# Conditioning vectors in PSUM banks 4 to 7 beside the first projections, and value transposes taking turns with the probability transposes

## The reference

```python
mod_x = silu(c) @ w_ada[l] + b_ada[l]        # 6 x 1024 values: shifts, scales, gates
mod_c = silu(c_ctx) @ w_ada[l] + b_ada[l]    # the same for the context tokens
hx = modulate(rmsnorm(x_lat, g_attn[l]), sh1x, sc1x)
aqx, akx, avx, bqx, bkx, bvx = split_cols(hx @ w_in[l])
# group A: 8 query heads on 2 key/value heads of 64, q and k rms-normalised, rotated
# group B: 4 heads, two 64-wide softmax maps each, values of 128, softmax(1) - lam * softmax(2)
x_lat = x_lat + g1x * (merge_heads(a_out_x, b_out_x, g_sub[l], lam_init) @ w_o[l])
# then an up-projection, a convolution of width 3, SiLU gate, a down-projection
```

## Time and profile before

| | us |
|---|---|
| median of 3 runs | 1796.95 |
| lowest and highest | 1795.91, 1799.62 |
| the profiled execution | 1795.55 |
| its span in the trace | 1793.7 |

### The profile page before, as it was taken

One profiled execution on the slowest core, in us unless ns is written; L12 is line 12 of the kernel. 1 busy time (PEld: TensorE's weight loads), 2 busy tenths in 40 slices (PEclk: granted clock), 3 DMA queues, 4 the chain that ended last, 5 costly groups with the idle time before them and its releaser, 6 DMA issues.

```text
span 1793.7 us, 26070 instructions
## 1 busy us (share of the span) xinstructions
PE 1674.4 (93%) x9610; PEld 1418.3 (79%) x9610; DVE 1135.6 (63%) x1744; ACT 768.8 (43%) x1267; POOL 629.8 (35%) x311
## 2 busy tenths in 40 slices
PE   5869998889999999999999998999878999999997
PEld 3757877668888888888888886787767888888887
DVE  6996767667877566667336674677654864254256
ACT  6526666445244321333123344665545443243242
POOL 0454652121113334322433317564122154444442
PEclk9988999899999999999999999999999999999999
DMA  9340000023313243343434422001012132332222
GB/s 387 113 139 24 24 25 24 13 92 147 103 50 127 83 138 119 114 132 110 157 109 130 152 94 93 16 24 35 24 35 88 54 106 94 103 96 94 94 94 94
DMA packets 45534, 168.24 MB, mean 94 GB/s; under 512 B 4736, under 2 KB 6784, under 8 KB 43520
## 3 DMA queue, kind: packets, MB, share of 16 engines
q1 hardware_dynamic: 40896, 156.48, 25.9%
q10 hardware_dynamic: 4544, 10.49, 1.6%
HBM read 161.71 MB, written 5.24 MB: 93 GB/s over the span
## 4 chain that ended last, share of the span: by engine, by line
PE 78%; DVE 11%; issue 5%; ACT 3%; DMA 2%; POOL 1%; SPq 0%; ACTq 0%; DVEq 0%; POOLq 0%
PE ps L1193 22%; PE ps L1194 22%; PE ps L1195 22%; PE ps L1315 4%; PE ps L1329 3%; DVE junk_lead L1990 2%; PE ps L1348 2%; DVE nb L2266 1%; PE ps L1349 1%; DVE p_sb L2284 1%; DVE pt_lo L2291 1%; PE ps L1139 1%; DMA ada_first<-first_d 1%; POOL w_lo L1075 1%; DVE ht L2105 1%
## 5 line engine op out<-in xcount | busy, mean ns | idle before, releaser
L1075 POOL TENSOR_TENSOR w_lo<-w_raw,w_hi 128x1024 fp32r<-128x1024 f32 x175 | 446.9, 2556 | 939.6 <-ACT w_hi L1588 939.5
L1193 PE MATMUL ps<-h_hi,w_hi 128*128 128x512 f32 (+1 forms) x1592 | 566.8, 356 | 9.4 <-DVE h_lo L2113 6.9
L1194 PE MATMUL ps<-h_lo,w_hi 128*128 128x512 f32 (+1 forms) x1592 | 556.5, 350 | 0.0
L1195 PE MATMUL ps<-h_hi,w_lo 128*128 128x512 f32 (+1 forms) x1592 | 556.0, 349 | 0.0
L1193 PEld LDWEIGHTS ps<-h_hi,w_hi 128*128 128x128 f32 x1592 | 303.1, 190 | 57.2 <-issue 19.0
L1195 PEld LDWEIGHTS ps<-h_hi,w_lo 128*128 128x128 f32 x1592 | 302.6, 190 | 39.7
L1194 PEld LDWEIGHTS ps<-h_lo,w_hi 128*128 128x128 f32 x1592 | 303.3, 191 | 35.9
L1588 ACT ACTIVATE w_hi<-w_raw 128x1024 fp32r<-128x1024 f32 x188 | 198.3, 1056 | 246.9 <-PE ps L1195 218.7
L1193 PE MATMUL ps<-a_hi,w_hi 128*128 128x512 f32 (+1 forms) x552 | 191.6, 347 | 1.2 <-DVE a_lo L2480 1.2
L1194 PE MATMUL ps<-a_lo,w_hi 128*128 128x512 f32 (+1 forms) x552 | 191.3, 347 | 0.0
L1195 PE MATMUL ps<-a_hi,w_lo 128*128 128x512 f32 (+1 forms) x552 | 191.0, 346 | 0.0
(11 more groups left out here) (173 smaller groups left out, 2467.1 us busy)
## 6 DMA issues: line engine op xcount, KB each, us to landing
w_raw<-w_d SPq DMA_DIRECT2D x188, 512.0 KB, 3.5
ada_b<-ada_d SPq DMA_DIRECT2D x56, 512.0 KB, 4.3
ada_first<-first_d SPq DMA_DIRECT2D x8, 1024.0 KB, 21.9
ada_lead<-ada_d SPq DMA_DIRECT2D x14, 512.0 KB, 3.5
ada_mid<-ada_d SPq DMA_DIRECT2D x10, 512.0 KB, 7.2
x_sb<-x_d SPq DMA_DIRECT2D x2, 1536.0 KB, 11.0
x_sb<-x_d ACTq DMA_DIRECT2D x1, 3072.0 KB, 11.4
x_spill_d<-x_sb ACTq DMA_DIRECT2D x1, 2048.0 KB, 7.5
```

The source lines that it names most:

```text
L1075: nc.gpsimd.tensor_tensor(w_lo[:, c % RING, :], w_raw[:, c % RAW, :], w_hi[:, c % RING, :].bitcast(f32), ALU.subtract).then_inc(w_lo_done, 1)
L1193: nc.tensor.matmul(out, lh, rh, start=first, stop=False)
L1194: nc.tensor.matmul(out, lh, rl_, start=False, stop=False)
L1195: return nc.tensor.matmul(out, ll, rh, start=False, stop=last)
```

## The change

1. **Conditioning in PSUM, layer 0.** ScalarE's silu moves into the loop of the first norm (`conditioning(k)`), a half at a time, with the table load at k = 1 and the spill at k = 4. It then copies each silu'd vector, 1024 columns, to PSUM: `c_held(0)` in banks 4 and 5 (k = 5), `c_held(1)` in banks 6 and 7 (k = 7). The 28 instructions of VectorE (`ada_ahead`) read the vector from there. The tiles have four buffers instead of two; the third and fourth lie where `c_bc` was, so their first loads wait for the spill and for both copies. SP's order of tile and unit loads is LEADS_AHEAD.
2. **Banks and order of the opening.** In layer 0 units 2 to 6 rotate over banks 0 to 2, head squares go to bank 3, and the values of A are transposed in bank 2 alone. Head factors wait for the last conditioning tile. All tiles have positions from -20 up, and SD, SR, RH, RL have -25 instead of -6, in both layers.
3. **Value transposes in turns, both layers.** `turn_beside` gives the two parts of a head B's value transposes two numbers in the sequence of T, so they use banks 4 and 5 in turn with the probability transposes. They come after the last T of item 0 for head 0, of A's last item with j = 2 for head 1, and of the last item of head B 0 and of head B 1 for heads 2 and 3 (`behind`), and before the first T of the item after it. Bank 7 holds projections alone. The operations of units 9 to 11 are made after A's items with j = 2 instead of after all of A.

```diff
+LEADS_AHEAD = [2, 2, 2, 3, 2, 3]
-def unit_banks(u):
+def unit_banks(l, u):
+    if l == 0:
+        return {0: (0, 1), 1: (2, 3), 2: (0, 1), 3: (2, 0), 4: (1, 2), 5: (0, 1), 6: (0, 1)}.get(u, (7, 7))
     return {0: (0, 1), 1: (2, 3), 2: (4, 5), 3: (6, 7), 4: (0, 1), 5: (2, 3), 6: (0, 1)}.get(u, (7, 7))
...
+    last_j = {j: [it["n"] for it in items if it["kind"] == "A" and it["j"] == j][-1] for j in range(A_HEADS // 2)}
+    behind = [0, last_j[2], at_b[1] - 1, at_b[2] - 1]
...
-            ada.append(op("DVE", "ada", 2.35, -20 + (c - 2 * KT) * .5, [], c=c))
+            ada.append(op("DVE", "ada", 2.6, -20 + (c - 2 * KT) * .5, [], c=c))
...
-            ada.append(op("DVE", "ada", 2.6, -3, [ada[-1]], c=c))
+            ada.append(op("DVE", "ada", 2.6, -20 + (c - 2 * KT) * .5, [ada[-1]], c=c))
-    sd = op("ACT", "SD", 1.7, -6, [y["ST"] for y in normed])
-    rc = op("DVE", "SR", 1.7, -6, [sd])
-    rh = op("ACT", "RH", .4, -6, [rc])
-    both = op("DVE", "RL", .45, -6, [rh])
+    sd = op("ACT", "SD", 1.7, -25, [y["ST"] for y in normed])
+    rc = op("DVE", "SR", 1.7, -25, [sd])
+    rh = op("ACT", "RH", .4, -25, [rc])
+    both = op("DVE", "RL", .45, -25, [rh])
-    bank_user = {0: units[2]["SQ"] + units[2]["EV"], 1: units[3]["SQ"] + units[3]["EV"]}
+    bank_user = {0: ada[-1:], 1: ada[-1:]}
+    if l > 0:
+        bank_user = {0: units[2]["SQ"] + units[2]["EV"], 1: units[3]["SQ"] + units[3]["EV"]}
...
-            turn_values(y, (7, 7), 0)
-            y["VH"][0]["need"] += home(y)
-            raw_free[u % 2] = [y["VT"][-1]]
+            raw_free[u % 2] = y["VT"] = []
+    def turn_beside(y, it):
+        nonlocal n_t
+        y["VH"], y["VL"] = [], []
+        for n, (k0, k1) in enumerate([(0, 4), (4, 6)]):
+            tid = n_t
+            n_t += 1
+            at = it["n"] + .9 + .05 * n
+            lo2, v2 = t_ops[tid - 2]["LOT"], v_ops[tid - 2]
+            vt = op("PE", "VT", .11 * (k1 - k0), at, y["EV"] + [lo2, it["T"][-1]] + y["VT"][-1:], y=y, n=n, k0=k0, k1=k1,
+                    bank=4 + tid % TURNS, before=dict(lo2=lo2))
+            vh = op("ACT", "VH", .62 if n == 0 else .4, at, [vt] + (home(y) if n == 0 else []), y=y, n=n, VT=vt, k0=k0, k1=k1,
+                    bank=4 + tid % TURNS)
+            vl = op("DVE", "VL", .68 if n == 0 else .42, at, [vh], y=y, n=n, VH=vh, k0=k0, k1=k1, bank=4 + tid % TURNS)
+            vt["LOT"] = vl
+            t_ops[tid], v_ops[tid] = vt, v2
...
+        for b in range(B_HEADS):
+            if behind[b] == n - 1:
+                turn_beside(units[B_TILE + 3 * b + 1], prev_item)
...
+    lead_home = [R_QKV + 28 * KB, R_QKV + 32 * KB, R_X + 24 * KB, R_X + 28 * KB]
+    ada_lead = [place(f"ada_lead{i}", [P, D], f32, lead_home[i]) for i in range(4)]
...
+    def c_held(s):
+        return ps[:, 4 + 2 * s:6 + 2 * s, :].rearrange("p a b -> p (a b)")
...
+            def load_lead(c):
+                n = c - FIRST_ADA
+                if 2 <= n < 4:
+                    sp.wait_ge(c_spilled, 16)
+                    sp.wait_ge(c_held_done, 2)
+                elif n >= 4:
+                    sp.wait_ge(ada_used, c - 3)
+                sp.dma_start(ada_lead[n % 4][:, :], ada_in[c, :, :]).then_inc(lead_loaded[n % 4], 16)
...
+            lead = FIRST_ADA
+            for c, n in zip(range(RING, wo_unit(0) + RING + RAW), LEADS_AHEAD):
+                for j in range(n):
+                    load_lead(lead + j)
+                lead += n
+                load_unit(c)
...
+            def conditioning(k):
+                if k == 1:
+                    act.wait_ge(c_loaded, 16)
+                    A(act_scrap[:, :], sm[:, 0:1], ACT.Silu)
+                if k in (2, 3):
+                    A(c_bc[:, k - 2, :], c_bc[:, k - 2, :], ACT.Silu).then_inc(c_ready, 1)
+                if k == 4:
+                    act.wait_ge(c_ready, 2)
+                    act.dma_start(c_spill, c_bc[:, :, :]).then_inc(c_spilled, 16)
+                if k == 5:
+                    A(c_held(0), c_bc[:, 0, :], ACT.Copy).then_inc(c_held_done, 1)
+                if k == KT - 1:
+                    A(c_held(1), c_bc[:, 1, :], ACT.Copy).then_inc(c_held_done, 1)
...
+            def ada_ahead(c):
+                n = c - FIRST_ADA
+                dve.wait_ge(lead_loaded[n % 4], 16 * (n // 4 + 1))
+                dve.wait_ge(ada_used, c)
+                for s in range(2):
+                    if n == 0:
+                        dve.wait_ge(c_held_done, s + 1)
+                    ins = V.tensor_tensor_reduce(junk_lead[:, :], ada_lead[n % 4][:, :], c_held(s), 1.0, 0.0,
+                                                 ALU.mult, ALU.add, mod[:, s, c:c + 1])
```

More of the change, by code:

```diff
@@ L177, in mixing_plan @@
                3: (at_b[2] - 1.4, at_b[3] - 1.3)}
-    units = [dict(u=u, c=in_unit(l, u), what=unit_kind(u), groups=unit_groups(l, u), banks=unit_banks(u))
+    units = [dict(u=u, c=in_unit(l, u), what=unit_kind(u), groups=unit_groups(l, u), banks=unit_banks(l, u))
              for u in range(IN_TILES)]
+    last_j = {j: [it["n"] for it in items if it["kind"] == "A" and it["j"] == j][-1] for j in range(A_HEADS // 2)}
+    behind = [0, last_j[2], at_b[1] - 1, at_b[2] - 1]
     bank = {}
@@ L283, in mixing_plan @@
     for y in normed:
-        y["ST"]["need"] += [units[2]["SQ"][-1], units[2]["EV"][-1]]
+        y["ST"]["need"] += [units[1]["EV"][-1]] if l == 0 else [units[2]["SQ"][-1], units[2]["EV"][-1]]
     ada = []
@@ L324, in mixing_plan @@
     v0 = units[1]
-    turn_values(v0, (2, 3), 0)
+    turn_values(v0, (2, 2) if l == 0 else (2, 3), 0)
     for x in v0["VT"] + v0["VH"] + v0["VL"]:
@@ L477, in mixing_plan @@
                 attention(it)
-        else:
+                if it["n"] == behind[1]:
+                    for u in range(9, 12):
+                        b_unit(u)
+        elif b > 1:
             for u in range(6 + 3 * b, 9 + 3 * b):
@@ L660, in backbone @@
     ada_junk = place("ada_junk", [P, D], bf16, R_O + 12 * KB)
-    ada_lead = [place(f"ada_lead{i}", [P, D], f32, R_QKV + (28 + 4 * i) * KB) for i in range(2)]
+    lead_home = [R_QKV + 28 * KB, R_QKV + 32 * KB, R_X + 24 * KB, R_X + 28 * KB]
+    ada_lead = [place(f"ada_lead{i}", [P, D], f32, lead_home[i]) for i in range(4)]
     junk_lead = place("junk_lead", [P, D], bf16, R_O + 16 * KB)
@@ L742, in backbone @@
         ada_loaded = [sem("ada_loaded0"), sem("ada_loaded1")]
+        lead_loaded = [sem(f"lead_loaded{i}") for i in range(4)]
+        c_held_done = sem("c_held_done")
         first_ada_loaded = [sem(f"first_ada_loaded{i}") for i in range(2 * FIRST_ADA // FIRST_GROUP)]
@@ L1004, in _ @@
             sp.dma_start(tabs[:, :, :], tab_in).then_inc(tab_loaded, 16)
-            a = FIRST_ADA
-            for j in range(2):
-                load_ada(a + j, first=True)
-            for j in range(RING):
-                load_unit(RING + j)
-                if j:
-                    load_ada(a + 2 * j)
-                    load_ada(a + 2 * j + 1)
-            for j in range(LEAD_MORE // 2):
-                load_unit(2 * RING + j)
-                load_ada(3 * KT + 2 * j)
-                load_ada(3 * KT + 2 * j + 1)
-            units(2 * RING + LEAD_MORE // 2, wo_unit(0) + RING + RAW)
+            lead = FIRST_ADA
[4 more added lines that the diff above has]
+                load_unit(c)
+            units(RING + len(LEADS_AHEAD), wo_unit(0) + RING + RAW)
             def load_mid(n):
@@ L1240, in wait_bank, with wait_turned @@
                         pe.wait_ge(v_lo_done, before["VL"]["no"])
+                    if "lo2" in before:
+                        wait_turned(before["lo2"])
+                def wait_turned(lo):
+                    pe.wait_ge(v_lo_done if lo["kind"] == "VL" else pt_lo_done, lo["no"])
                 def project(x):
@@ L1259, in head_squares @@
                     y = x["y"]
-                    pe.wait_ge(squared, last_no(y["SQ"] + units[2]["SQ"]))
-                    pe.wait_ge(proj_copied, last_no(units[2]["EV"]))
+                    pe.wait_ge(squared, last_no(y["SQ"] if l == 0 else y["SQ"] + units[2]["SQ"]))
+                    pe.wait_ge(proj_copied, last_no(units[1 if l == 0 else 2]["EV"]))
+                    bank = 3 if l == 0 else 4
                     n = y["place"]
@@ L1264, in head_squares @@
                     for b in range(y["width"] // BLOCK):
-                        mm = nc.tensor.matmul(ps[b * QUAD:(b + 1) * QUAD, 4, 0:BLOCK], sel,
+                        mm = nc.tensor.matmul(ps[b * QUAD:(b + 1) * QUAD, bank, 0:BLOCK], sel,
                                               a_sq[n % 2][:, b * BLOCK:(b + 1) * BLOCK], start=n == 0,
@@ L1324, in turn @@
                     if x["lo_before"]:
[L1325 removed]
+                        wait_turned(x["lo_before"])
                     else:
```

49 lines of the change are left out of this document (23 added, 26 removed).

## The result

The changed kernel takes 1764.19 us (median of 4 runs, 1762.90 to 1764.74), the kernel before beside it 1796.53: ratio 0.9815, 95% interval 0.9801 to 0.983. The forecast was 1769, 1755 to 1786. So the time lies 5 us under the forecast and inside case (a)'s own range. One of the four executions of a later kernel (two buffers, old load order) took 2094.62 us at a mean granted clock of 0.745; its ratio is taken from the other three.

A forecast was written before the change was run, and what follows sets the result against it. TensorE, busy 93% of the span, bounds the kernel, so only its idle or slow-clock stretches give time. Terms -15.5 - 1 - 7 - 3 - 1 = -27.5 on 1795.6 give 1768.1, 1769 as median; range 1755 to 1786.

The forecast's parts named there:

- case (a): Whole kernel: the time comes out as summed, 1769 us, with its own range 1759 to 1777; likeliest, 57%.
- Conditioning at 1220 ns: Layer 0's opening: each of VectorE's 28 conditioning instructions takes 1220 ns with a PSUM input, mean 1827 before; -17.0 us.
- SP 15.5 us earlier: Layer 0's opening: spreading of the head norms starts at 116.0 instead of 131.55, set by TensorE, not VectorE.
- Late loads, -1.6: Layer 0's opening: four buffers instead of two remove TensorE's wait for a_sq behind a late weight load; -1.6 us.
- The clock, -1: Layer 0, from SP to the first scores: half the work lost at the lower clock comes back; -1 us (0 to -2).
- Part 1 as a whole: Layer 0's opening: conditioning from PSUM starts SP 15.5 us earlier, plus 1 us of clock; -16.5 us on the total.
- Part 2, -11: Value transposes leaving bank 7: -7 us in layer 0 (unit 14 earlier), -3 in layer 1, -1 at unit 10.
- New turns cost 0 to +1 a place: Heads B: waits added by value transposes taking turns in banks 4 and 5; 0 to +1 us a place, inside the ranges.
- (b): Heads B: bank 7's hold was hidden anyway, fillers move and later waits grow; 1780 us, 17%.
- (c): Conditioning: the PSUM operand doesn't free VectorE, SP stays at 131; 1786 us, or 1797 if the turns fail too; 9%.
- (e): Heads B: slower, because the transposes' turns add waits at 8 places; 1821 us at 5 us a place; 5%.
- (d): Whole kernel: more than summed, a hole filled early keeps the clock up and additions run bare; 1757 us or less, 12%.

The follow-up runs named there:

- two buffers, old load order: Changed kernel with two conditioning-load buffers instead of four and the earlier kernel's load order on SP's queue, vectors still from PSUM: 1763.06 us, ratio 0.9808.
- the order alone: Kernel before, with its last six conditioning tiles behind head_both and their loads behind those of units 9 and 10, vectors in SBUF: 1798.47 us, ratio 1.001.
- unit 14 held: Changed kernel, but in both layers unit 14's first projection waits until unit 13's value halves are written: 1773.2 us, ratio 0.9867.
- conditioning alone: Changed kernel with the value transposes of heads B back in bank 7 and in their old order, both layers: 1786.91 us, ratio 0.9938.
- the turns alone: Kernel before plus only the value transposes in turns and the new place of units 9 to 11: 1776.87 us, ratio 0.9887.
- the vector in SBUF: Against the kernel with two conditioning buffers and the new load order (1772.05 us), the 28 conditioning instructions read the vector from SBUF: 1786.99 us, ratio 0.9949.
- turns in layer 1 only: Changed kernel, but layer 0 keeps its value transposes in bank 7: 1774.74 us, ratio 0.9868.
- unit 17 held: Changed kernel, but in both layers unit 17's first projection waits until unit 16's value halves are written: 1770.54 us, ratio 0.9847.

## Why the prediction was right, point by point

- **Conditioning at 1220 ns: right.** 28 times 1218 ns, 34.1 us after 51.2, is the forecast -17.0 to 0.1 us. The Trainium skill, "SBUF — State Buffer", section "SBUF: two separate sides", has the exclusive lock; the pair of kernels that differ in this operand alone agrees with it (45.7 against 34.1 us). The Trainium skill, "VectorE: DVE Perf Modes", section "The TRN2 errata", charges a PSUM source 62 cycles more. It is not seen: the 16 unstretched instructions from SBUF took 1207 to 1227 ns, the 28 from PSUM 1200 to 1223. The a_raw additions, for which nothing was counted, did get shorter: 4.3 us instead of 7.8.
- **SP 15.5 us earlier: right within 1.2.** 131.55 to 115.95 and 115.8. Counted from the first unit it is 14.3 to 15.0, since that unit started up to 1.4 us earlier. The bank wait was 1.80 (forecast 1.9). That TensorE and not VectorE sets SP held: SP starts without a wait.
- **Late loads, -1.6: the wait went, but not for the reason given.** Of the 2.0 us for which TensorE waited for a_sq before the head squares nothing is left. But nothing is left of them with two buffers in the old order either. There too ScalarE's w_hi waits for no load up to 132, where it waited for 10.9 us before. The likely reason is that SP's queue gets to the weights in time once VectorE is faster; with the order alone, vectors in SBUF, the 2.0 us are there again. The four buffers only make good what the new order would cost; the 1.0 to 1.7 us between those two kernels is another matter (a wait of 1.0 us for va is in the one with two buffers alone).
- **ScalarE's moved pieces, unit 5's load: nothing, as said.** The first unit starts no later in any kernel that has them.
- **The clock, -1: about right at its place.** The step from the first to the second pair of scores took 8.7 and 9.2 us instead of 10.2, with 0.3 more from SP to the scores. The clock did not stay at 1.00 through 120, though (0.96).
- **Part 1 as a whole, -16.5 with the clock: mis-sized.** 11 measured. The first score came 14 us earlier, counted from the first unit, but the saving was taken to last to the end, and it did not: in the profiled execution 4.3 us went in L0 to L1 and 2.4 in layer 1's scores. What the sum leaves out is that a stage that is reached earlier can meet longer pauses, with falls of the clock behind them. In layer 1's scores of this kernel the clock stands at 0.50 in two windows of five us, where the lowest before is 0.66.
- **Part 2, -11: mis-sized the other way.** 20 measured. Layer 0: -7 and a share of -1 forecast, 10 to 11 measured. Layer 1: -3 and the rest of -1 forecast, 10 measured. Two steps failed. In layer 0 the forecast took the score chain to gain 13 us at head B 2 and to keep 7 of it at head B 3, whose scores wait for unit 17. Instead the steps to both got shorter, by 7 and by 8 us (22.8 to 15.8 and 30.4 to 22.6, each from two pairs earlier), after the steps before them had lost 2.7. Unit 17's own hold, which got no price, is 4 us of it. The scores of head B 2 did not come within 5 us of the pair before, as forecast, but 12.2 us behind it. In layer 1 the step to the scores of head B 2 went from 26.1 to 17.0 us and is back at 26.8 with unit 14 held, though only 4.6 us of that are left at the last scores: at its own place the hold was worth 9 us where 3 had been counted, from a window whose TensorE looked busy (15.37 of 20 us). Unit 17's hold is only 0.7 of layer 1's 10, and with both holds tried some 5 us of the 10 have no place that a run shows.
- **New turns cost 0 to +1 a place: right in sum.** The step that follows the first turns in layer 0 is 10.6 us instead of 5.6, but by the 25th pair the scores are level with those of the kernel with conditioning alone. In layer 1 TensorE waits once for vb_lo:

```profile
1258.95 0.76 PE L1377 MATMUL ps<-sm,p_sb 128*128 128x128 f32 x4 [2.96 <-DVE vb_lo L2331]
```

- **Rivals.** (b), bank 7's hold hidden: refuted by the turns alone (-20) and by unit 14 held (+9). (c): refuted by the vector in SBUF. (e): TensorE's longest wait at a turn is 2.96 us, and the sum is a gain. (d), more than summed, holds for part 2 taken alone, though its reasons (the clock, the bare additions) were not separated; part 1's loss hid it.

What stays open: why the clock falls in one execution and not in the other, the reload's 7.7 us, and the 5 us of layer 1's 10 that neither hold explains (unit 10's hold was not tried alone).

## What to carry to other kernels

When VectorE's instruction is longer than its shortest brother, lay GpSimd beside it. If both inputs are in SBUF, moving one to PSUM can give the time back; here it cost nothing in the instruction itself (1218 ns), but PSUM banks, and with them a wait of 1.80 us at unit 2. In a queue that waits in order, count what stands behind a waiting load: its price showed two engines away. Price a removed hold at every place where it stands, by the distance between the stages that wait (scores to scores), not only by how idle the engine in between looks. A right total is no proof of its terms: run each part alone, and look whether an early saving is lost again at later pauses and clock falls.

## What the runs showed of the hardware

- The same program can differ by 2.8 us in one stretch between two executions, with the granted clock falling at other moments. Three of the kernels profiled (conditioning alone, turns in layer 1 only, unit 17 held) had an additional fall behind a pause of over 3 us; behind the 1.24 us pause of before and the 1.73 us of unit 14 held there was none. The changed kernel's first execution had a short one (0.66 in five us) behind 1.80 us.
- GpSimd's products with the rotation tables hold up a VectorE instruction with two SBUF inputs as its w_lo does: 2.25 us each in the rows above, and VectorE ends 1.08 us after.
- The five a_raw additions, which keep two SBUF inputs, take 3.4 us together with two buffers, 4.3 in the changed kernel, 7.8 before it and 9.8 with the order alone, though nothing about them was edited.
